# Interleaving the high and low halves of split weights in two of three SBUF buffers

## The reference

```
z = h @ w_in                                  # 1024 x 5320, three mixers and their gates
merged @ w_out                                # 1024 x 1024
(gelu(conv(a)) * g) @ w_down                  # a, g = split(h @ w_up); 1024 x 5632, 2816 x 1024
x @ gla_w_in, (o * silu(g)) @ gla_w_out       # second block, layer 0
x @ w_kv, x @ swa_w_in, o @ swa_w_out         # second block, layer 1
```

## Time and profile before

| | |
|---|---|
| runs | 746.07, 746.49, 753.45 us; median 746.49 |
| profiled execution, its own time | 748.46 us |
| its span in the trace | 746.7 us |
| PE busy | 721.3 us (97%), 5900 matmuls |
| PEld busy | 702.3 us (94%), 5900 loads |
| DVE, ACT busy | 522.7 us (70%), 395.9 us (53%) |
| granted TensorE clock | 0.995 of full speed over the span |

### The profile page before, as it was taken

The page is one execution under the profiler, slowest core; times in us unless marked ns, Lnnn a source line. Parts: engine busy times, 40 slices in busy tenths (PEclk is TensorE's granted clock), DMA queues, the critical chain, the costliest instruction groups (busy, mean ns, idle before and its releaser), DMA issues.

```text
span 746.7 us, 14086 instructions
## 1 busy us (share of the span) xinstructions
PE 721.3 (97%) x5900; PEld 702.3 (94%) x5900; DVE 522.7 (70%) x763; ACT 395.9 (53%) x564; POOL 106.3 (14%) x90
## 2 busy tenths in 40 slices
PE   8899999998999999999999999999999999999995
PEld 6789899897898999999999989999999999999995
DVE  4879878876888777787777656936674456556665
ACT  4197454554364555445445347646555455556552
POOL 0040000000520200000001230000005265443000
PEclk9999999999999999999999999999999999999998
DMA  8995575566364355656565634534446544333101
GB/s 342 410 362 173 226 283 206 197 257 232 124 226 170 115 190 205 206 190 212 212 269 215 230 111 171 180 141 143 160 164 244 199 171 144 123 129 114 57 1 57
DMA packets 22265, 141.13 MB, mean 189 GB/s; under 512 B 2389, under 2 KB 3029, under 8 KB 6458
## 3 DMA queue, kind: packets, MB, share of 16 engines
q1 hardware_dynamic: 21626, 137.28, 50.7%
q0 software_dynamic: 576, 2.95, 1.0%
HBM read 139.17 MB, written 1.05 MB: 188 GB/s over the span
## 4 chain that ended last, share of the span: by engine, by line
PE 70%; DVE 12%; issue 6%; ACT 6%; DMA 4%; POOL 1%; SPq 0%; DVEq 0%; ACTq 0%
PE res L1593 20%; PE res L1594 20%; PE res L1595 20%; ACT wsplit L640 4%; DVE wsplit L1056 3%; DVE raw L1069 2%; PE pX L1796 2%; DMA shared<-in_w_ada 2%; DMA raw<-in_wts 1%; PE pS L1776 1%; DVE shared L1069 1%; DMA y<-in_w_ada 1%; ACT sq L655 1%; PE pS L1829 1%; PE pT L1786 1%
## 5 line engine op out<-in xcount | busy, mean ns | idle before, releaser
L1593 PE MATMUL res<-hs,wsplit 128*128 128x256 f32 (+1 forms) x1120 | 317.5, 283 | 3.2 <-DVE wsplit L1056 1.5
L1594 PE MATMUL res<-hs,wsplit 128*128 128x256 f32 (+1 forms) x1120 | 311.7, 278 | 0.0
L1595 PE MATMUL res<-hs,wsplit 128*128 128x256 f32 (+1 forms) x1120 | 311.5, 278 | 0.0
L1056 DVE TENSOR_TENSOR wsplit<-raw,wsplit 128x2048 fp32r<-128x2048 f32 (+3 forms) x101 | 226.7, 2248 | 117.7 <-ACT wsplit L640 108.1
L640 ACT ACTIVATE wsplit<-raw 128x2048 fp32r<-128x2048 f32 (+3 forms) x101 | 188.2, 1865 | 104.3 <-issue 74.5
L1593 PEld LDWEIGHTS res<-hs,wsplit 128*128 128x128 f32 (+1 forms) x1120 | 209.3, 187 | 4.7 <-issue 2.3
L1594 PEld LDWEIGHTS res<-hs,wsplit 128*128 128x128 f32 (+1 forms) x1120 | 209.3, 187 | 0.4
L1595 PEld LDWEIGHTS res<-hs,wsplit 128*128 128x128 f32 (+1 forms) x1120 | 209.0, 187 | 0.2
L538 POOL TENSOR_TENSOR sq<-sq,rope 128x512 f32<-128x512 f32 x18 | 39.5, 2195 | 78.3 <-ACT sq L655 78.3
L1595 PE MATMUL res<-us,wsplit 128*128 128x256 f32 x176 | 48.6, 276 | 0.0
L1593 PE MATMUL res<-us,wsplit 128*128 128x256 f32 x176 | 48.6, 276 | 0.0
(11 more groups left out here) (336 smaller groups left out, 1213.8 us busy)
## 6 DMA issues: line engine op xcount, KB each, us to landing
raw<-in_wts SPq DMA_DIRECT2D x97, 1024.0 KB, 5.0
raw<-in_w_ada SPq DMA_DIRECT2D x16, 1024.0 KB, 5.4
shared<-in_w_ada SPq DMA_DIRECT2D x6, 1024.0 KB, 11.9
gates<-in_wts SPq DMA_DIRECT2D x4, 768.0 KB, 13.3
raw<-in_wts SPq DMA_DIRECT2D x4, 768.0 KB, 5.3
y<-in_w_ada SPq DMA_DIRECT2D x2, 1024.0 KB, 9.3
x<-in_xT SPq DMA_DIRECT2D x2, 512.0 KB, 4.5
gv<-in_ln_rows POOLq DMA_DIRECT2D x1, 1024.0 KB, 7.6
```

Of the source, the lines that this page charges most:

```text
L1056: nc.vector.tensor_tensor(halves(c)[:, 1, 0:b], raw[RAW_OF["w", c] % RAW][:, 0:b], halves(c)[:, 0, 0:b].bitcast(f32), ALU.subtract).then_i ...
L1593: mm(out, a[:, 0, :], b[:, 0, :], start=first, stop=False)
L1594: mm(out, a[:, 1, :], b[:, 0, :], start=False, stop=False)
L1595: return mm(out, a[:, 0, :], b[:, 1, :], start=False, stop=last)
```

## The change

The buffers of two slots keep high and low values in alternating columns: column 2n is high value n, column 2n+1 is low value n. In slot 2 this pattern begins 16 floats (64 bytes) into the buffer, which is made 64 bytes longer. Slot 0 is as before. Chunks whose weights move (the second kind above) keep the old `[high | low]` form in all slots. `halves` returns the same view in both cases (partition, part, column), with a step of one or of two floats between columns.

```
+PAIRED = (None, 0, 16)
...
-        wsplit = [sb(f"wsplit{i}", [P, 2, CW], f32r) for i in range(SPL)]
+        wsplit = [sb(f"wsplit{i}", [P, 2 * CW + (PAIRED[i] or 0)], f32r) for i in range(SPL)]
...
-            return wsplit[c % SPL][:, :, :]
+            at = PAIRED[c % SPL]
+            if at is None or c in (VA, VB) or GV <= c < GG or SV <= c < SWA or c >= GOUT and c < SK or c >= SOUT:
+                return wsplit[c % SPL][:, 0:2 * CW].rearrange("p (e n) -> p e n", e=2)
+            return wsplit[c % SPL][:, at:at + 2 * CW].rearrange("p (n e) -> p e n", e=2)
```

## The result

The changed kernel takes 762.58 us, the median of 3 runs (762.45 to 763.94), against 746.49 us (746.07 to 753.45): 1.0191 times as long by the means, 95% interval 1.0141 to 1.0240. The run of 753.45 us among the three of before pulls that ratio down; by the medians it is 1.0216. I had said 739 us. The time lies inside the range of 729 to 764 us, near its upper end, on the other side of no change: 16.1 us up instead of 7.4 us down. The profiled execution has a span of 760.8 us against 746.7 us, so 14.1 us have to be found in it.

The account below looks back on a forecast made before the run. It took PE to be the bound, its matmul pace held by weight loads. Profiled 748.5 us less 7.4 us for interleaved loads, nothing for the 64 bytes or writes, gave 741.1; less 2.0 for the median, 739 us; range 729 to 764 us.

Parts of the forecast that it names:

- What bounds the kernel: Whole kernel: PE is busy for 97% of the span, and the weight load, one per matmul, holds the loop.
- Loads of interleaved columns ... I take 113.3 ns: 58 interleaved chunks, 2,712 matmuls: all go at 113.3 ns, so the 1,656 at 117.8 ns gain 7.4 us.
- Its upper bound, 120.0 ns or 10.7 us: Interleaved chunks: at the worst pace seen with full loads, 120.0 ns, 10.7 us would be lost.
- its weakest point: Interleaved weight loads: a load at a step of two might be slower by itself, which no earlier row could exclude.
- The 64 bytes ... I take nothing and keep both: Tensors behind `wsplit` move by 64 bytes: counted as nothing, between 6.8 us lost and 5.8 us gained.
- The bound on the slow side: Slot 0 and moving chunks: if 128 bytes is the step that counts, 5.3 us and 1.5 us lost, 6.8 us.
- multiples of 128: `ys` against `wsplit`, `wgo` against `gos`: distances that are multiples of 128 bytes go with the slow 120.0 ns pace.
- ACT's and DVE's writes at nothing: Split writes at a two-float step: counted as costing nothing.
- The bound of 20 us: Split writes: if both engines' writes double, DVE becomes the bound and up to some 20 us are lost.
- The sum: Profiled execution 748.5 us - 7.4 = 741.1 us; median 2.0 us lower, so 739 us.
- The third, with the shift's loss on top: Interleaved loads lose slack, collisions reach the loop: 120.0 ns, 757 us, with the 64-byte move's loss 764 us; chance 0.17.
- Rival 2: All matmuls: pace is a state of PE, not of the reads; nothing moves, 746.5 us; chance 0.10.

## Why the prediction was wrong, step by step

- *What bounds the kernel* was right: the load in the loop, and the pace of matmuls is all that moved. PE's waits stayed at 1.6 us and the clock at 1.00.
- *"Loads of interleaved columns ... I take 113.3 ns"* is the step that failed. Measured: 120.0 to 121.6 ns in the up and down products of the whole kernel in four layouts, and 120.0 to 122.3 alone. The term is 12.2 us lost instead of 7.4 us gained; in the kernel without the shift, where nothing but the form of these chunks has changed, it is 1,056 x 8.2 + 1,656 x 2.9 = 13.5 us. Its upper bound, 120.0 ns or 10.7 us, came from contiguous loads and was nearly right for another reason. My argument (two streams of the same rate keep out of each other's way) looked at how load and stream meet, and took it that the load by itself is as fast as ever. It is not: 117.8 ns instead of 111.7 ns with hardly any stream beside it. The prediction names that as its weakest point, and gave it too little chance.
- The rule of the Trainium skill that I weighed there (Advanced Engine Details and Errata, SBUF Cachelines) asks for at least two hits on a line of 16 bytes. I read it as "two are enough", by which the load keeps its speed. The runs show 5% lost at exactly two, 55% at a step of three and twice the time at four. The direction is the page's; that two hits are enough is not borne out.
- *"The 64 bytes ... I take nothing and keep both"* was mis-sized. The bound on the slow side, which I kept for the range, had the mechanism (distance to `hs`, period 128): measured 118.7 ns in place of the assumed 120.0, 3.2 + 1.4 = 4.6 us against 6.8 us. For the whole kernel in the old layout it is 10.1 us. That 128 bytes give the time back supports the period, though not exactly: alone, 128 bytes off has 118.7 ns where 0 has 120 or more, 96 is as slow as 0, and a layout moved by 128 has other paces outside the up and down products. The prediction's rule ("multiples of 128") was drawn from pairs that leave one out: `dos` lies 32 bytes off a multiple of 128, by the addresses given ahead of it, and had 120.0 ns too.
- *ACT's and DVE's writes at nothing* was right on the path: DVE is unchanged, ACT 0.2 us a chunk, all beside other work. The bound of 20 us was not needed.
- *The sum* would have been 748.5 + 12.2 + 3.2 + 1.4 = 765.3 us for the profiled execution, which had 762.6. Of the 2.7 us between, 2.4 are idle time of PE, which fell from 746.7 - 721.3 = 25.4 to 760.8 - 737.8 = 23.0 us at the slower pace, and 0.3 are in the means.
- *The rivals.* The third, with the shift's loss on top, came true in its number: 764 us against 762.58. I gave it 0.17 in all. Its mechanism is right in that the interleaved load has lost its slack, wrong in that it takes a collision for the cause: 117.8 of the 120 ns are there with hardly a stream beside the load. So that the time lies inside the range is in part luck. Rival 2 (the pace is a state of PE) is half right for contiguous weights: the level is a state, set by what ran before, but within what the addresses allow. The Trainium skill's statement that PE waits on nobody (SBUF — State Buffer, Who interferes with whom) is not borne out, if it is read to cover PE's own two reads: 64 unused bytes cost 1.3%.
- What stays open: why neighbours with interleaved weights push slot 0 off the good level at one offset and not at another (117.8 and 113.3 ns), what in a load and a stream meets at some distances and not at others, and why one program enters its up and down products now at one level and now at the other. A layout that alternates in blocks of four high and four low values, whose load would span as much but in whole runs, was not tried; in all runs here the bytes that a load spans and the step between its weights go together, so which of the two counts is not shown.

## What to carry to other kernels

In a loop that is bound by weight loads, keep the weights of a load contiguous: even a two-float step, which DVE reads for nothing, has a floor of its own above the contiguous pace. Treat every change of a tensor's size as a change of all addresses behind it, and run the shift by itself before believing in the rest. Where one row of the trace shows a pace of a form and none shows the form of the change, a bound from neighbouring rows isn't a forecast; price the instruction by itself first.

## What the runs showed of the hardware that I had not expected

- A load's time goes with the bytes that it spans once these are over 512: 117.8, 173.4 and 233.2 ns for 1,024, 1,536 and 2,048 bytes, and 111.7 ns for 512. At a granted clock of 0.50 the widest one still takes 233 ns, while the one of 1,024 bytes takes 213.
- The same matmuls on the same data keep 113.3 or 117.8 ns for a whole stage by how they were entered, and three matmuls ahead can turn it either way. In this kernel that is worth 7 us, the distance between the two groups of runs of one and the same program.
- 64 unused bytes in the middle of the layout cost 10.1 us of 746; 128 cost nothing.
- Of two engines that write at a two-float step one pays (ACT 10%, 1,910 to some 2,100 ns) and one doesn't (DVE, 2,303 to 2,301 ns).
